# Attention steps of neighbouring items gathered at one weave point, in three attentions of a two-block transformer kernel

## The reference

```python
s = jnp.einsum('bhqd,bhkd->bhqk', qi, kt).astype(jnp.float32) * scale
s = jnp.where(kpos[None, :] <= qpos[:, None], s, -jnp.inf)
p = jax.nn.softmax(s, axis=-1).astype(vt.dtype)
return jnp.einsum('bhqk,bhkd->bqhd', p, vt)
```

```python
alpha = jax.nn.softmax(jnp.stack(lses, axis=0), axis=0)
o = jnp.sum(alpha[..., None] * jnp.stack(outs, axis=0).astype(jnp.float32), axis=0)
```

## Time and profile before

| | |
|---|---|
| median of 3 runs | 4263.91 us (4260.83 to 4265.5) |
| the profiled execution | 4269.24 us, span 4267.4 us |
| PE busy | 3973.2 us, 93% of the span |
| PE weight loads | 3191.0 us, 75% |
| DVE busy | 2339.2 us, 55% |
| ACT busy | 1290.6 us, 30% |
| POOL busy | 837.4 us, 20% |
| mean granted TensorE clock | 0.945 of full |
| chain that ended last | PE 80%, DVE 14%, ACT 3%, issue 2% |

### The profile page before, as it was taken

The page is one execution under the profiler, slowest core; times in us unless marked ns, Lnnn a source line. Parts: engine busy times, 40 slices in busy tenths (PEclk is TensorE's granted clock), DMA queues, the critical chain, the costliest instruction groups (busy, mean ns, idle before and its releaser), DMA issues.

```text
span 4267.4 us, 48366 instructions
## 1 busy us (share of the span) xinstructions
PE 3973.2 (93%) x19416; PEld 3191.0 (75%) x19416; DVE 2339.2 (55%) x3017; ACT 1290.6 (30%) x1687; POOL 837.4 (20%) x580
## 2 busy tenths in 40 slices
PE   7997899999869999999888999999999999999998
PEld 6665688776658887887667788788867778777886
DVE  2668655538756555557556533743554544446334
ACT  3343322324423322222453222322232323222222
POOL 2122255322215454654322000000000000000000
PEclk7998899989879999999998999999999999998998
DMA  3111244421205454553222233233312212112331
GB/s 117 60 50 60 81 142 145 122 63 52 69 30 161 135 148 117 154 138 111 62 61 63 79 99 99 77 101 99 98 58 67 65 57 67 53 52 67 101 99 60
DMA packets 556442, 377.74 MB, mean 89 GB/s; under 512 B 30121, under 2 KB 553866, under 8 KB 556218
## 3 DMA queue, kind: packets, MB, share of 16 engines
q1 hardware_dynamic: 555642, 372.55, 29.7%
q10 hardware_dynamic: 576, 2.10, 0.1%
HBM read 372.44 MB, written 2.17 MB: 88 GB/s over the span
## 4 chain that ended last, share of the span: by engine, by line
PE 80%; DVE 14%; ACT 3%; issue 2%; SPq 0%; DMA 0%; DVEq 0%; ACTq 0%
PE bank L437 56%; PE bank L473 4%; PE bank L445 4%; DVE w_lo L415 3%; PE bank L809 2%; PE bank L793 2%; PE bank L1923 2%; PE bank L1948 1%; ACT w_hi L406 1%; PE bank L1968 1%; PE bank L801 1%; DVE hgrn_scores L1265 1%; DVE k_decayed L1279 1%; DVE norm_tmp L1451 1%; DVE q_decayed L1279 1%
## 5 line engine op out<-in xcount | busy, mean ns | idle before, releaser
L437 PE MATMUL bank<-H_hi,w_hi 128*128 128x512 f32 (+1 forms) x2368 | 969.7, 410 | 0.2
L415 DVE TENSOR_TENSOR w_lo<-w_raw,w_hi 128x2048 fp32r<-128x2048 f32 (+3 forms) x285 | 732.7, 2571 | 359.6 <-ACT w_hi L406 352.3
L437 PE MATMUL bank<-H_hi,w_lo 128*128 128x512 f32 (+1 forms) x2368 | 928.8, 392 | 0.0
L437 PE MATMUL bank<-H_lo,w_hi 128*128 128x512 f32 (+1 forms) x2368 | 927.8, 392 | 0.0
L406 ACT ACTIVATE w_hi<-w_raw 128x2048 fp32r<-128x2048 f32 (+3 forms) x285 | 529.1, 1857 | 301.7 <-DMA w_raw<-in_ffn_w_up 131.7
L437 PE MATMUL bank<-U_hi,w_hi 128*128 128x512 f32 x1408 | 559.8, 398 | 24.4 <-DVE U_lo L1126 16.9
L437 PEld LDWEIGHTS bank<-H_hi,w_hi 128*128 128x128 f32 (+1 forms) x2368 | 446.4, 189 | 151.7 <-issue 67.2
L437 PE MATMUL bank<-U_hi,w_lo 128*128 128x512 f32 x1408 | 552.7, 393 | 0.0
L437 PE MATMUL bank<-U_lo,w_hi 128*128 128x512 f32 x1408 | 552.4, 392 | 0.0
L437 PEld LDWEIGHTS bank<-H_hi,w_lo 128*128 128x128 f32 (+1 forms) x2368 | 446.3, 188 | 97.8 <-issue 0.5
L437 PEld LDWEIGHTS bank<-H_lo,w_hi 128*128 128x128 f32 (+1 forms) x2368 | 447.3, 189 | 87.7 <-issue 6.3
(11 more groups left out here) (332 smaller groups left out, 5132.2 us busy)
## 6 DMA issues: line engine op xcount, KB each, us to landing
w_mod_raw<-in_w_mod SPq DMA_DIRECT2D x144, 512.0 KB, 6.3
w_raw<-in_ffn_w_gate SPq DMA_DIRECT2D x88, 512.0 KB, 4.0
w_raw<-in_ffn_w_up SPq DMA_DIRECT2D x88, 512.0 KB, 5.3
w_raw<-in_dil_w_in SPq DMA_DIRECT2D x36, 1024.0 KB, 5.1
w_raw<-in_w_mlp_in SPq DMA_DIRECT2D x32, 1024.0 KB, 5.5
w_raw<-in_w_mlp_out SPq DMA_DIRECT2D x32, 1024.0 KB, 5.3
w_raw<-in_ffn_w_down SPq DMA_DIRECT2D x32, 1024.0 KB, 5.3
w_raw<-in_w_in SPq DMA_DIRECT2D x16, 1024.0 KB, 5.3
```

Of the source, the lines that this page charges most:

```text
L415: dve.eng.tensor_tensor(WL[u % SLOTS][:, 0:n], RAW[u % SLOTS][:, 0:n], WH[u % SLOTS][:, 0:n].bitcast(F32), ALU.subtract).then_inc(lo_done. ...
L437: mm = pe.eng.matmul(bank[0:m, :], w[:, k, c0:c0 + m], r[:, k, :], start=(k == 0 and i == 0), stop=(k == kt - 1 and i == 2))
```

## The change

Four edits, all in the order of steps.

1. A new helper `att_together` gives all that stands at one point for s: turn of item s-2, values of s-3, scores of s, divide of s-1. The mixer's attention puts 35 such groups at 35 points instead of 128 steps one by one.
2. `mla_steps` returns the same groups, 12 for each part and 15 for the last, and `mla_at` puts each whole group at one point.
3. `dil_steps` returns groups: turn of item s-1, values of s-2, a mix if there is one, scores of s. The bias, the keys' step and the stats stay alone.
4. The six mixes of a set of heads no longer follow the stats in the same chunk. They stand in the groups of the next chunk (g = 0 of the next `hq`), one for each of s = 0 to 5. Only those of the last set stay where they were.

```diff
+        def att_together(s, n):
+            return [("turn", s - 2)] * (2 <= s < n + 2) + [("values", s - 3)] * (s >= 3) + [("scores", s)] * (s < n) + [("divide", s - 1)] * (1 <= s < n + 1)
...
-            n, todo = ATT_HEADS * NB, []
+            n = ATT_HEADS * NB
             for s in range(n + 3):
-                todo += [("scores", s)] * (s < n) + [("divide", s - 1)] * (1 <= s < n + 1) + [("turn", s - 2)] * (2 <= s < n + 2) + [("values", s - 3)] * (s >= 3)
-            for j, step in enumerate(todo):
-                put(ATT_FROM + (2 * j + 1) * (MIX_POINTS - ATT_FROM) // (2 * len(todo)), step)
+                put(ATT_FROM + (2 * s + 1) * (MIX_POINTS - ATT_FROM) // (2 * (n + 3)), *att_together(s, n))
...
-            n, out = 3 * MLA_HEADS, []
...
+            n = 3 * MLA_HEADS
+            return [att_together(s, n) for s in range(12 * part - 12, n + 3 if part == 4 else 12 * part)]
...
-            for j, step in enumerate(todo):
-                where[(2 * j + 1) * points // (2 * len(todo))].append(step)
+            for j, steps_ in enumerate(todo):
+                where[(2 * j + 1) * points // (2 * len(todo))].extend(steps_)
...
-            steps_ = [("bias", half) for half in range(1 if g else 2)] + [("keys", j) for j in range(0 if g else 2)]
+            mixes = [("mix", k) for k in range(6)]
+            steps_ = [[("bias", half)] for half in range(1 if g else 2)] + [[("keys", j)] for j in range(0 if g else 2)]
             for s in range(n + 2):
-                steps_ += [("scores", s)] * (s < n) + [("turn", s - 1)] * (1 <= s < n + 1) + [("values", s - 2)] * (s >= 2)
+                mixed = mixes[s:s + 1] if g == 0 and hq and s < 6 else []
+                steps_.append([("turn", s - 1)] * (1 <= s < n + 1) + [("values", s - 2)] * (s >= 2) + mixed + [("scores", s)] * (s < n))
             if g == 2:
-                steps_ += [("stats", 0)] + [("mix", k) for k in range(6)]
+                steps_ += [[("stats", 0)]] + ([[m] for m in mixes] if c == CHUNKS else [])
...
                 if s == 0:
+                    pe.eng.wait_ge(dil_vt_used.sem, dil_vt_used.taken["pe"])
                     pe.eng.wait_ge(dil_f.sem, dil_f.next(pe))
```

More of the change, by code:

```diff
@@ L1842, in dil_steps @@
                 return []
-            g, _ = dil_parts(c - 1)
+            g, hq = dil_parts(c - 1)
             n = 4 if g else 8
-            steps_ = [("bias", half) for half in range(1 if g else 2)] + [("keys", j) for j in range(0 if g else 2)]
+            mixes = [("mix", k) for k in range(6)]
+            steps_ = [[("bias", half)] for half in range(1 if g else 2)] + [[("keys", j)] for j in range(0 if g else 2)]
             for s in range(n + 2):
-                steps_ += [("scores", s)] * (s < n) + [("turn", s - 1)] * (1 <= s < n + 1) + [("values", s - 2)] * (s >= 2)
+                mixed = mixes[s:s + 1] if g == 0 and hq and s < 6 else []
+                steps_.append([("turn", s - 1)] * (1 <= s < n + 1) + [("values", s - 2)] * (s >= 2) + mixed + [("scores", s)] * (s < n))
             if g == 2:
-                steps_ += [("stats", 0)] + [("mix", k) for k in range(6)]
+                steps_ += [[("stats", 0)]] + ([[m] for m in mixes] if c == CHUNKS else [])
             return steps_
@@ L1854, in dil_at @@
             where = [[] for _ in range(points)]
-            for j, step in enumerate(todo):
-                where[(2 * j + 1) * points // (2 * len(todo))].append(step)
+            for j, together in enumerate(todo):
+                where[(2 * j + 1) * points // (2 * len(todo))].extend(together)
             return where
@@ L2053, in dil_act @@
                         dil_act_step(act, c - 1, step)
-            for step in dil_steps(CHUNKS):
-                dil_act_step(act, CHUNKS - 1, step)
+            for together in dil_steps(CHUNKS):
+                for step in together:
+                    dil_act_step(act, CHUNKS - 1, step)
             act_linear(act, ("dil_out",), running_squares(("dil_out",), y_tile), later=True, early=lin[("dil_out",)][:-1])
@@ L2128, in dil_dve_step @@
                 t, n = divmod(s, 3)
+                if g == 0:
+                    hq -= 1
                 if s == 0:
@@ L2154, in dil_dve @@
                         dil_dve_step(dve, c - 1, step)
-            for step in dil_steps(CHUNKS):
-                dil_dve_step(dve, CHUNKS - 1, step)
+            for together in dil_steps(CHUNKS):
+                for step in together:
+                    dil_dve_step(dve, CHUNKS - 1, step)
             sandwich_next(dve, 1, 1)
```

## The result

The changed kernel takes 4404.95 us (median of four runs, 4398.68 to 4413.19) against 4264.7 us for the kernel before on the same chip: 1.0331 of it, 95% interval 1.0315 to 1.0348. It is 140 us slower. The forecast was +93, to 4357 us, with a range that ended at 4405, where the measured time lies. The direction was right, and so was the place of the new waits; what they cost through the clock was priced far too low.

The account below looks back on a forecast made before the run. PE, busy 93% of the span, was taken to bound the kernel. Terms -16.5 - 31 + 40 + 16 + 57 + 20 + 12 = +97.5 gave 4361 us, taken as 4357 (+93) for overlapping waits; range 4290 to 4405.

Parts of the forecast that it names:

- What is late next is the turn: In all attentions, turns stand nearer to what they need and wait; MLA +40 us, mixers +16, dilated +57 and +20.
- the two-point gaps: Mixers: nine of 34 gaps between groups have two points, each 0.37 us short for the division; 3.3 us per layer.
- Dilated group 0, +57: Dilated attention, group 0: turns wait for the chain from bias to exponential, splits and mixes; 11.9 us first set, 15.0 others.
- the rest, +20: Dilated attention: turn waits in group 2 (2.7 us four times), group 1 (0.6 four times) and last chunk (7); +20 us.
- Moving the mixes, -31: Dilated attention: three factor waits go (-17 us), the slow clock behind them (-7), most of the bias wait (-7).
- Joining, -16.5: Turn, values and scores at one point save matmul seams: dilated -16 us, mixers -0.5, as little in MLA; range -8 to -20.
- The clock, +12: Dilated attention: eight new waits of 2.9 us and more lower the clock, 1.5 us lost at each; +12 us.
- -7 from the moves: Dilated attention: half-speed work behind three factor waits, 2.3 us lost each time, goes with them; -7 us.
- Half the waits: Rival: item waits partly fall together; MLA, mixers and group 0 cost half, 4300 us; chance 0.18.
- Faster: Rival: the chain from scores to turn fits the gap everywhere, so only savings count; -47.5, 4216 us; chance 0.07.
- even: Rival, milder form of the faster one: waits at a fifth of their price, time comes out even; chance 0.05.
- The clock rival: Rival: one-microsecond waits in every MLA group lower the clock, matmuls there take 46 us more; 4403 us; chance 0.10.

Follow-up runs that it names:

- e1_divide_first: Changed kernel with the division of item s-1 put ahead of the scores and maximum of item s in mixers and MLA; 4346.8 us, 1.0206 of before.
- f2_moves_only: Kernel before with only the mixes moved into the next chunk, every step at its own point; 4244.9 us, 0.9961 of before.
- f7_half_filled: Changed kernel with 420 thrown-away matmuls added ahead of the turns' wait for the probabilities; 4342.9 us, 1.0195 of before.
- f1_dil_lag_only: Kernel before with only the dilated attention changed: joined groups, turn one item later than in the changed kernel, mixes in next chunk; 4238.2 us, 0.9948 of before.
- e4_turn_apart: Changed kernel with the dilated attention's turn alone, half a gap behind its group; 4371.4 us, 1.0263 of before.

## Why the prediction was right in kind and wrong in size

- **What is late next is the turn, by 0.3 to 3 us.** Right. The turns' waits lead the list, MLA's stretch idles 37 us more where the stage as a whole was to grow by 40, and e1_divide_first shows the cause named. MLA's window of 204 us, forecast at about 244, is 248 (2116.3 to 2364.4). The mixers were priced at +8 of waiting each and idle 7.5 and 6.6 more, but the first one's window of 169 us, forecast at 177, is 187 (137.3 to 324.4). The waits there are almost all at the splits (2.5 to 3.7 us, four per layer, and 1.6 at the first turn); the two-point gaps, priced at 0.37 each, waited 0.2.
- **Dilated group 0, +57; the rest, +20.** The idle time of the stage grew by 42.8, with 26 us of old waits gone from it (17.7 for the factors, 8.1 for the bias): 68 us of new waiting at the turns against 77. Group 0 has 52.7 of its 57 (11.8 us in the first set, 13.6 or 13.7 in the others); the last chunk has 3.8, where 7 were named for it.
- **Moving the mixes, -31.** The factor waits and the slow stretch behind them went as priced (-24), and in the changed kernel the bias wait fell by 8. By themselves (f2_moves_only) the moves give 17, because there the bias wait stays and values wait 5.1 us. In the changed kernel not even that was seen: the chunks in which group 0 is woven with mixes are 26 to 29 us longer than before's, three times, where the first set's, without mixes, is 13 longer; the two group 2 chunks read that gave up their mixes are 13 and 16 shorter.
- **Joining, -16.5.** 10 us by PE's busy time. Within the -8 to -20 named.
- **The clock, +12, and -7 from the moves.** This is the step that failed. The forecast had PE's own work at -16.5 - 7 + 12 = -11.5 us. It came out at +46.7 in the four stretches, 58 us off: 29 in the dilated attention, 20 in the mixers, 9 in MLA. The waiting, by contrast, was forecast at 40 + 16 + 57 + 20 - 24 = 109 and measured at 94. Not all of the 58 is clock. The joins gave 10 where 16.5 stood. And part is drawing: a matmul of 256 columns is drawn 0.28 us long but the next one starts 0.12 after it (2167.15 and 2167.27 above); where PE waits behind it, all 0.28 count as busy. With 77 more turns waiting than before (96 against 19), at 0.16 us each, that is an estimated 12 us. What is left for the clock is 46.7 + 10 - 12, about 45 us by this estimate, where the sum had +12 - 7 = +5. The sum had a clock term for the eight waits of 2.9 us and more in the dilated attention alone, and none for the mixers, although the splits' waits of 2 to 2.8 us stood priced beside it: the mixer's window had kept its 0.97 in the trace, and that was read as if it would keep it with longer waits. f7_half_filled shows the cause: 69 us of the changed kernel's time goes when fillers for 61% of its waits are put in and nothing else is altered. Some of that the kernel before loses as well, so the 69 are no price for the change.
- **The rivals.** Half the waits: refuted, 94 of 109 us are there. Faster and even: refuted for the change as it stands; with the longer lag the dilated half of it is faster. The clock rival gave 4403, close to the result, but for the wrong place: MLA, with a wait in nearly every group, has 0.94 in its stretch before and after. By the Trainium skill ("TensorE: Matmul & The Clock Gate", section "A second HAM failure mode: psum-queue depth-cycling") MLA's many brief pauses should have moved the clock. This trace does not bear that out: behind MLA's waits of 2.50 and 2.52 us the clock is 0.76, and in the 53 us between, with ten waits of up to 1.8 us at the turns, it is 1.00. By these windows the fewer, longer waits are what lowers it, with the exceptions named there.

Left open: MLA's busy time grew by 8.9 us at an unchanged mean clock. Some 2.8 us of it are the missing 0.06 of the clock over 46 us more. The drawing of matmuls ahead of a wait gives an estimated 5.4 (47 turns wait instead of 13). In e1_divide_first, where 14 wait, the busy time is down to 208.4 us at the same 0.94, so the excess does go with the waits; a run that tells the two parts from each other was not made.

## What to carry to other kernels

A step that is moved nearer to what it needs is priced on the other engines' queues: ask what stands in front of its producer there, and whether that in turn waits for this engine. The whole chain from first to last step must fit in the lag; shifting the middle only passes the wait on. Price a new wait on TensorE twice, as a wait and by the clock behind it, where it is as long as those here that lowered the clock (2.5 to 3.7 us in the windows shown), and check the answer in the busy time of matmuls whose number hasn't changed.

## What the runs showed of the hardware that was not expected

- Matmuls that are thrown away can pay: 420 of them, 94 us of work placed in waits, brought the clock from 0.936 to 0.957 and the time from 4411.6 to 4342.9 us. Twice as many, more than the waits could hold, gave back less (4370.5).
- A matmul of 128x128 f32 by the constant tile shows as two records, 0.112 us apart, where each transpose shows as one. The products of scores, values and mask, f32 as well, also show as two records each.
- Identical code differs between profiled executions by its clock: the untouched part between the two mixers takes 538.7 us in before at a clock of 0.92 and 532.5 in f1_dil_lag_only at 0.94, and the changed kernel's second mixer 270.5 us in one profile and 279.8 in e4_turn_apart's. A stage's gain is better read from its own stretch than from the span.
